# Computing 12 of 16 gate tiles inside two attention stages instead of in the matmul chains behind them

## What is computed

```python
# first block
proj = h @ w_in[layer]
p_rwkv, p_diff, p_gate = jnp.split(proj, [RWKV_COLS, RWKV_COLS + DIFF_COLS], axis=-1)
o_rwkv = rwkv7_mix(p_rwkv, ...) @ rwkv_w_o[layer]
o_diff = diff_attention(p_diff, ...) @ diff_w_o[layer]
gates = jax.nn.sigmoid(p_gate).reshape(bsz, seqlen, N_BRANCH, D_MODEL)
merged = gates[:, :, 0] * o_rwkv + gates[:, :, 1] * o_diff
h_res = h_res + merged @ w_out[layer]
# second block
o = nsa_attention(q, k_cmp, v_cmp, k_s, v_s, k_w, v_w, nsa_gates, rel_bias)
y = jax.nn.sigmoid(mg[..., :d]) * y_conv + jax.nn.sigmoid(mg[..., d:]) * y_attn
x = x + y @ w_out[i]
```

## Time and profile before

| | us |
|---|---|
| median of 3 runs | 3678.36 |
| lowest, highest | 3672.93, 3681.27 |
| profiled execution, its span | 3676.3 |

### The profile page before, as it was taken

The page is one execution under the profiler, slowest core; times in us unless marked ns, Lnnn a source line. Parts: engine busy times, 40 slices in busy tenths (PEclk is TensorE's granted clock), DMA queues, the critical chain, the costliest instruction groups (busy, mean ns, idle before and its releaser), DMA issues. The chain is left out here.

```text
span 3676.3 us, 57266 instructions
## 1 busy us (share of the span) xinstructions
PE 3363.3 (91%) x24193; PEld 2748.5 (75%) x24193; DVE 2025.1 (55%) x3289; ACT 1230.3 (33%) x2142; POOL 203.8 (6%) x171
## 2 busy tenths in 40 slices
PE   7978999988999999888999998978699889999998
PEld 6868888956888888656677776866578587878886
DVE  4875654565355344577546776356736545464342
ACT  4542332254334233214433222234412234233231
POOL 2213220010000000000000000000100020000000
PEclk9989998988999999989999999989799889999999
DMA  4431103201322222520122222312022003233231
GB/s 147 156 124 48 48 19 116 69 1 52 97 93 92 98 92 80 145 72 13 47 75 92 86 86 93 99 59 93 13 92 95 1 2 109 78 106 98 93 97 58
DMA packets 99462, 287.84 MB, mean 78 GB/s; under 512 B 19738, under 2 KB 23962, under 8 KB 97160
## 3 DMA queue, kind: packets, MB, share of 16 engines
q1 hardware_dynamic: 93104, 269.43, 22.6%
q10 hardware_dynamic: 6104, 14.75, 1.6%
HBM read 264.22 MB, written 19.89 MB: 77 GB/s over the span
## 5 line engine op out<-in xcount | busy, mean ns | idle before, releaser
L240 PE MATMUL acc<-h_hi,whi 128*128 128x512 f32 x1992 | 800.5, 402 | 65.4 <-DVE wlo L432 43.0
L240 PE MATMUL acc<-h_hi,wlo 128*128 128x512 f32 x1992 | 791.1, 397 | 0.0
L240 PE MATMUL acc<-h_lo,whi 128*128 128x512 f32 x1928 | 770.0, 399 | 0.0
L240 PEld LDWEIGHTS acc<-h_hi,whi 128*128 128x128 f32 x1992 | 379.1, 190 | 176.0 <-DVE wlo L432 45.3
L338 DVE TENSOR_TENSOR wlo<-wbuf,whi 128x1024 fp32r<-128x1024 f32 (+3 forms) x277 | 318.6, 1150 | 272.9 <-ACT whi L256 270.5
L240 PEld LDWEIGHTS acc<-h_hi,wlo 128*128 128x128 f32 x1992 | 379.3, 190 | 87.8
L240 PEld LDWEIGHTS acc<-h_lo,whi 128*128 128x128 f32 x1928 | 366.8, 190 | 86.2 <-issue 2.9
L256 ACT ACTIVATE whi<-wbuf 128x1024 fp32r<-128x1024 f32 (+3 forms) x277 | 274.5, 991 | 347.4 <-PE acc L240 318.3
L240 PE MATMUL acc<-arena_round,whi 128*128 128x512 f32 x736 | 236.6, 392 | 4.8 <-DVE arena_round L398 4.8
L338 DVE TENSOR_TENSOR wlo<-ahead,whi 128x1024 fp32r<-128x1024 f32 (+3 forms) x132 | 152.3, 1154 | 140.9 <-ACT whi L256 140.2
L256 ACT ACTIVATE whi<-ahead 128x1024 fp32r<-128x1024 f32 (+3 forms) x132 | 131.4, 995 | 174.7 <-PE acc L240 168.3
(11 more groups left out here) (748 smaller groups left out, 6265.7 us busy)
## 6 DMA issues: line engine op xcount, KB each, us to landing
wbuf<-in_mlp_out SPq DMA_DIRECT2D x46, 512.0 KB, 3.3
wbuf<-in_mlp_in SPq DMA_DIRECT2D x45, 512.0 KB, 3.3
wbuf<-in_w_gates SPq DMA_DIRECT2D x38, 512.0 KB, 3.4
wbuf<-in_ffn_up SPq DMA_DIRECT2D x29, 512.0 KB, 3.3
wbuf<-in_w_qkv SPq DMA_DIRECT2D x23, 512.0 KB, 3.4
rwkv_factors<-factors SPq DMA_DIRECT2D x8, 1320.0 KB, 4.6
ahead<-in_mlp_in SPq DMA_DIRECT2D x19, 512.0 KB, 3.4
wbuf<-in_w_rwkv SPq DMA_DIRECT2D x18, 512.0 KB, 5.7
```

The source lines that it names most:

```text
L240: mm = nc.tensor.matmul(acc[t % NB][:, 0:T], wt[s % ring][:, k - a, :], xt, start=(kx == 0 and q == 0), stop=(kx == job.K - 1 and q == 2))
```

## The change

A new class `Beside` computes the first 12 gate tiles of a block step by step inside the attention that comes before the chain. Its function `made(step)` says how many of the 12 x 24 matmuls are done by the end of a step: in `diff_attention` 12 in each swap step and 6 in each score step, in `nsa_attention` 6 in each step. Weight tiles are split in halves of 4 squares: high part by ACT, two or three steps ahead (`high`), low part by POOL (`low`). PE does its share (`pe`) right after the step's scores or swaps and before `turn` and `weigh`. Sums are in a single bank `acc`; the eviction, by ACT in block one and by DVE with the scale in block two, writes the gate without its sigmoid. SP loads through two places (`sp_first`, `sp`, `sp_last`), the last load being the first tile of the following chain. The chains keep four gate tiles each, and a side object `LateSigmoid` takes the 12 sigmoids, three in each of the first four slabs; DVE waits for all of them at slab 3. All `warm` calls of both attentions go. To make room for the bank, `diff_attention` gives up `ps_v` (values go through `ps_t`, with two more waits) and `nsa_attention` has three banks of scores instead of four. In SBUF, the gates lie over tiles of `p` and `z` that are no longer needed, `unscaled` lies in `o`, and five constants of the rwkv stage are freed earlier.

```diff
@@ -99,6 +99,106 @@
 def tile_list(ap):
...
+class Beside:
+    def __init__(self, nc, w, x, out, ahead, following, made, ring, scale=None):
+        self.nc, self.w, self.x, self.out, self.following, self.scale = nc, w, x, out, following, scale
+        self.place, self.first_loaded, self.times = ahead
+        self.made, self.N, self.R = made, len(out), ring
+        self.issued = self.split = self.lowered = self.kept = 0
+    def prepare(self, s):
+        self.wbuf = [self.place, s.sb("wbuf", [P, 8, P])]
+        self.whi, self.wlo = ([s.sb(n, [P, 4, P], F32R) for _ in range(self.R)] for n in ("whi", "wlo"))
+        self.acc = s.ps("acc", [P, BANK])
+        self.w_loaded = [s.sem("w_loaded") for _ in range(2)]
+        self.hi_ready, self.lo_ready, self.w_used, self.evicted = (s.sem(n) for n in ("hi_ready", "lo_ready", "w_used", "evicted"))
+    def sp_first(self, sp):
+        if self.times == 1:
+            sp.dma_start(self.wbuf[0][:], self.w[0, 0]).then_inc(self.first_loaded, 16)
+        sp.dma_start(self.wbuf[1][:], self.w[1, 0]).then_inc(self.w_loaded[1], 16)
+    def sp(self, sp, start, stop):
+        for n in range(start, stop):
+            sp.wait_ge(self.lo_ready, 2 * n - 2)
+            sp.dma_start(self.wbuf[n % 2][:], self.w[n, 0]).then_inc(self.w_loaded[n % 2], 16)
+    def sp_last(self, sp):
+        n = self.following.shape[3]
+        sp.wait_ge(self.lo_ready, 2 * self.N)
+        sp.dma_start(self.place[:, 0:n, :], self.following[0, 0]).then_inc(self.first_loaded, 16)
+    def pe(self, pe, step):
+        while self.issued < self.made(step):
+            n, k, q = self.issued // 24, self.issued % 24 // 3, self.issued % 3
+            h = 2 * n + k // 4
+            if n > 0 and k == 0 and q == 0:
+                pe.wait_ge(self.evicted, n)
+            if k % 4 == 0 and q == 0:
+                pe.wait_ge(self.lo_ready, h + 1)
+            wt = (self.whi, self.whi, self.wlo)[q][h % self.R]
+            mm = self.nc.tensor.matmul(self.acc[:], wt[:, k % 4, :], self.x[1 if q == 1 else 0][k], start=(k == 0 and q == 0), stop=(k == 7 and q == 2))
+            if k % 4 == 3 and q == 2:
+                mm.then_inc(self.w_used, 1)
+            self.issued += 1
+    def high(self, act, step):
+        while self.split < 2 * self.N and 12 * self.split < self.made(step):
+            h, n = self.split, self.split // 2
+            if h % 2 == 0:
+                act.wait_ge(*((self.first_loaded, 16 * self.times) if n == 0 else (self.w_loaded[n % 2], 16 * ((n + 1) // 2))))
+            if h >= self.R:
+                act.wait_ge(self.w_used, h - self.R + 1)
+            self.nc.scalar.activation(self.whi[h % self.R][:], self.wbuf[n % 2][:, 4 * (h % 2):4 * (h % 2) + 4, :], ACT.Copy).then_inc(self.hi_ready, 1)
+            self.split += 1
+    def low(self, pool, step):
+        while self.lowered < 2 * self.N and 12 * self.lowered < self.made(step):
+            h = self.lowered
+            pool.wait_ge(self.hi_ready, h + 1)
+            self.nc.gpsimd.tensor_tensor(self.wlo[h % self.R][:], self.wbuf[h // 2 % 2][:, 4 * (h % 2):4 * (h % 2) + 4, :],
+                                         self.whi[h % self.R][:].bitcast(F32), ALU.subtract).then_inc(self.lo_ready, 1)
+            self.lowered += 1
+    def complete(self, step):
+        while self.kept < self.N and 24 * (self.kept + 1) <= self.made(step):
+            self.kept += 1
+            yield self.kept - 1
+    def evict_scaled(self, dve, n):
+        dve.wait_ge(self.w_used, 2 * n + 2)
+        self.nc.vector.tensor_tensor(self.out[n], self.acc[:], self.scale[:], ALU.mult).then_inc(self.evicted, 1)
+    def evict(self, act, n):
+        act.wait_ge(self.w_used, 2 * n + 2)
+        self.nc.scalar.activation(self.out[n], self.acc[:], ACT.Copy).then_inc(self.evicted, 1)
+class LateSigmoid:
+    def __init__(self, nc, x, slabs):
+        self.nc, self.x, self.slabs = nc, x, slabs
+    def prepare(self, s_, evicted_d):
+        self.done = s_.sem("sigmoid_done")
+    def pe(self, pe, s, stat):
+        pass
+    def act(self, act, s):
+        if s < self.slabs:
+            N = len(self.x)
+            for t in self.x[N * s // self.slabs:N * (s + 1) // self.slabs]:
+                self.nc.scalar.activation(t, t, ACT.Sigmoid).then_inc(self.done, 1)
+    def dve(self, dve, s):
+        if s == self.slabs - 1:
+            dve.wait_ge(self.done, len(self.x))
@@ -1527,7 +1627,7 @@
-def diff_attention(nc, c, p, o, subln, busy):
+def diff_attention(nc, c, p, o, subln, beside):
@@ -1550,10 +1650,11 @@
-        unscaled, junk = s.sb("unscaled", [P, NA, P]), s.sb("junk", [P, P])
+        unscaled, junk = o.rearrange("p i (j d) -> p (i j) d", d=P), s.sb("junk", [P, P])
...
-        ps_t, ps_m, ps_o, ps_v = (s.ps(n, [P, BANK]) for n in ("ps_t", "ps_m", "ps_o", "ps_v"))
+        ps_t, ps_m, ps_o = (s.ps(n, [P, BANK]) for n in ("ps_t", "ps_m", "ps_o"))
+        beside.prepare(s)
@@ -1588,10 +1689,12 @@
             def _(sp):
...
+                beside.sp_first(sp)
+                beside.sp(sp, 2, beside.N)
+                beside.sp_last(sp)
...
             def _(pe):
-                warm(nc, ps_m, busy, 10)
@@ -1604,9 +1707,10 @@
                 def values(i):
...
+                        pe.wait_ge(wt_copied, NJ * i - 2)
...
                     for j in range(NJ):
-                        mm = nc.tensor.transpose(ps_v[:, j * P:(j + 1) * P], p[:, i + 16, M + j * P:M + (j + 1) * P], c["ident"][:])
+                        mm = nc.tensor.transpose(ps_t[:, j * P:(j + 1) * P], p[:, i + 16, M + j * P:M + (j + 1) * P], c["ident"][:])
@@ -1630,6 +1734,7 @@
+                    pe.wait_ge(vt_copied, min((a + 2) // NJ, 7) + 1)
@@ -1649,7 +1754,7 @@
                 def scaled(a):
...
-                    bank = (ps_t, ps_v)[i % 2]
+                    bank = (ps_t, ps_m)[i % 2]
@@ -1659,12 +1764,13 @@
-                for i, a, _, a2, a3 in lagging():
+                for u, (i, a, _, a2, a3) in enumerate(lagging()):
...
+                    beside.pe(pe, u)
@@ -1679,7 +1785,7 @@
-                    nc.scalar.activation(vt[b][:].rearrange("p j d -> p (j d)"), ps_v[:], ACT.Copy)
+                    nc.scalar.activation(vt[b][:].rearrange("p j d -> p (j d)"), ps_t[:], ACT.Copy)
@@ -1704,7 +1810,8 @@
-                for i, a, _, a2, a3 in lagging():
+                for u, (i, a, _, a2, a3) in enumerate(lagging()):
+                    beside.high(act, u + 2)
@@ -1713,22 +1820,28 @@
+                    for n in beside.complete(u):
+                        act.wait_ge(swap_ready, 2 * (n // 2) + 2)
+                        act.wait_ge(cos_done, 2 * (n // 2) + 2)
+                        beside.evict(act, n)
...
                 for i in range(8):
...
-                    nc.scalar.activation(o[:, i, :], (ps_t, ps_v)[i % 2][:], ACT.Copy, scale=weight[:, i:i + 1]).then_inc(written, 1)
+                    nc.scalar.activation(o[:, i, :], (ps_t, ps_m)[i % 2][:], ACT.Copy, scale=weight[:, i:i + 1]).then_inc(written, 1)
...
             def _(pool):
                 for i in range(8):
...
+                    beside.low(pool, 5 * i - 3)
...
+                beside.low(pool, 5 * 8)
@@ -2105,8 +2218,9 @@
-        ps_s = [[s.ps("ps_s", [P, BANK]) for _ in range(2)] for _ in range(2)]
+        ps_s = [s.ps("ps_s", [P, BANK]) for _ in range(3)]
...
+        beside.prepare(s)
@@ -2126,8 +2240,10 @@
             def _(sp):
+                beside.sp_first(sp)
                 for i in range(4):
...
+                        beside.sp(sp, 3 * i - 4, 3 * i - 1)
@@ -2136,6 +2252,8 @@
                         for b in range(8):
...
+                beside.sp(sp, 8, beside.N)
+                beside.sp_last(sp)
@@ -2144,13 +2262,13 @@
-                    for e in range(2):
-                        if p > 1:
-                            pe.wait_ge(top_ready[e], p - 1)
-                    warm(nc, ps_s[0][p % 2], busy, 14 if p == 0 else 4 if br == 2 else 1)
+                    if p > 1:
+                        pe.wait_ge(top_ready[1], p - 1)
+                    if p > 0:
+                        pe.wait_ge(top_ready[0], p)
                     for e in range(2):
...
-                        nc.tensor.matmul(ps_s[e][p % 2][:, 0:n], qs[rows(e), i, qi * P:(qi + 1) * P], k, start=True, stop=True).then_inc(sc_ready[e], 1)
+                        nc.tensor.matmul(ps_s[(2 * p + e) % 3][:, 0:n], qs[rows(e), i, qi * P:(qi + 1) * P], k, start=True, stop=True).then_inc(sc_ready[e], 1)
@@ -2197,6 +2315,7 @@
                 for p in range(NP + 6):
...
+                        beside.pe(pe, p)
@@ -2210,6 +2329,7 @@
             def _(act):
...
+                beside.high(act, 1)
@@ -2242,11 +2362,16 @@
                 for p in range(NP + 7):
...
+                        beside.high(act, p + 3)
...
+            @block.gpsimd
+            def _(pool):
+                beside.low(pool, NP)
@@ -2267,7 +2392,7 @@
```

(46 more changed lines are left out.)

4 lines of the change are left out of this document (2 added, 2 removed).

## The result

| | before | after |
|---|---|---|
| median of 4 runs (range) | 3677.7 us (3672.9 to 3681.3) | 3618.4 us (3615.7 to 3621.7) |
| ratio (95% interval) | | 0.984 (0.9826 to 0.9854) |
| span of the profiled execution | 3676.3 us | 3613.9 us |

The change makes the kernel 59 us faster. The forecast was 3624, its range 3600 to 3657.

What follows compares the result with a forecast made beforehand. The prediction took TensorE (PE), 91% busy, to bound the kernel. Its terms, -133.4 + 49 - 4 + 28 + 6.3 = -54 us, gave 3624 us, with a range of 3600 to 3657.

Steps and rivals of the forecast that it cites:

- Part 1: The two chains: twelve of sixteen gate tiles leave each, 66.7 us a chain, -133.4 us for two blocks.
- Part 2: Differential attention: 288 gate matmuls come in and partly fill PE's holes; stage 176.7 against 127.7 us, +49 (38 to 64).
- insertions: Differential attention: 40 breaks of PE's run of plain float matmuls, 0.1 us each, 4 us (0 to 8).
- cold clock: Opening of each attention stage: PE starts at a low clock, 3 us each (1.5 to 7 and 0 to 6).
- own work: PE's time in a stage without waits, tails, dummy matmuls and lost clock: 96 us in differential, 102.0 in selected attention.
- Part 3: Start of chain 1: with the new early weight load PE idles less before its first gate matmul, -4 us (-4.3 to -3.5).
- Part 4: Selected attention: gate matmuls replace dummy ones and fill waits; stage 179.7 against 151.5 us, +28 (19 to 41).
- Part 5: Chain 2: ConvNorm blocks ACT in slab 3, so PE waits 7.9 us instead of 1.6 before slab 6, +6.3 (4 to 9.5).
- Steps are chains: Both attention stages: no wait shrinks, since gates before turn and weigh pass their full length on; 3661 us, chance 0.12.
- Slower by 0.4 an insertion: Both attention stages: each of 88 insertions costs 0.4 us, 35 in place of 4; 3692 us, chance 0.04.
- Clean filling: Both attention stages: insertions, evictions and POOL cost nothing; 3602 us, chance 0.17.
- POOL on the path: Selected attention: 24 low parts hold DVE up by 0.6 us each, +11 on the forecast; 3635 us, chance 0.10.

Runs made afterwards that it cites:

- e2: The kernel after, with 8 of 16 gate tiles inside the attention stages instead of 12: 3617.2 us.
- e3: The kernel after, with 14 of 16 gate tiles inside the attention stages and ConvNorm one slab earlier: 3610.8 us.
- e8: The kernel after, with each step's gate matmuls in two places, the last three behind the turning: 3615.3 us.
- e5: The kernel after, with the accumulator's eviction ahead of the copy of turned weights in each step instead of behind it: 3618.5 us.
- e4: The kernel after, with ConvNorm's block in chain 2 taken apart: root in slab 3, reciprocal in 4, products and SiLUs in 4, 6, 8, 10: 3612.8 us.
- e7: The kernel after, with each of POOL's 48 low parts computed three times in a row: 3644.6 us.
- e9: The kernel after, with each step's gate matmuls behind turning and weighing instead of between scores and turning: 3629.6 us.
- e1: The kernel before, with the matmuls that only keep TensorE busy taken out of both attention stages: 3702.3 us.

## Why the prediction was right, point by point

- **PE is the bound, and its holes can be filled.** Right. e2 and e3 show where it ends: with 8 tiles the first stage is full (146.3 of 147.9 us busy), with 12 both nearly.
- **Part 1, -133.4.** The way from chain 1 to the selected attention lost 72.5: 66.7, the 5.1 of the fourteen `warm`, and 0.7. The way to the first GELU lost 59.6, which is 66.7 less the new stall of chain 2 (6.2) and 0.9.
- **Part 2, +49.** It was +44.7. To the point at which the forecast ended the stage, 1.1 later than my mark, it is 172.4 instead of 176.7. The terms behind PE's own work were mis-sized: insertions 4, measured 0 (e8); evictions 5, measured 1.9 in rows and 3.5 by e5; cold clock 3, measured 2 (4 us at 0.50); POOL 2, of which no wait over 0.4 is to be seen. These are some 8 too much. On the other side, "own work" of 96 was some 4 too small; where these lie is open. (Its two estimates, 97.4 and 94.4, should by their own terms read 97.8 and 94.6, which explains little of it.)
- **Part 3, -4.** PE's idle time before chain 1 fell by 3.8. The stretch as a whole lost 5.9. The rest is in the thin steps: 24.4 us with 18.5 busy at a clock of 0.72 before (861.6 to 886), 22.3 with 17.2 busy at 0.85 after (903.7 to 926.0). That clock differs from trace to trace, so this part is luck.
- **Part 4, +28.** It was +27.3 from the end of the opening matmuls (146.8 and 5.1 before, 179.2 after). Evictions 5, measured 4.4; cold clock 3, measured 1.6 (4 us at 0.60). Own work and POOL, 102.0 and 3 in the sum, measure 106.5 together and are not separated. DVE was to come to 116 us of busy time and came to 125: the 9 us of POOL's hold that the sum left out of DVE. The sum was right because errors of both signs met.
- **Part 5, +6.3.** The wait is 7.8, forecast 7.9; against 1.6 before that is +6.2, forecast +6.3. The three sigmoids ahead of the root take 1.66, and the rows are those that the prediction named. e4 shows what stands in ACT's block of 8.9 us: 3.35 of it is DVE's reciprocal, and taking the rest apart leaves a wait of 3.8.
- **What hides the moved work.** Halves split ahead: no wait for POOL's low parts in the kernel after; e7 shows that the lead is used up when they take three times as long. The shared `ps_t`: hidden, and e9 shows the price without the gate matmuls ahead.
- **The rivals.** *Steps are chains*: no; the waits of the two stages went from 33.5 to 7.7 us. *Slower by 0.4 an insertion*: no, by e8. *Clean filling*, 3602: the insertions are indeed free, but evictions aren't. Its three terms at nothing give 3605, not 3602, which is the case of all low ends. *POOL on the path*: the mechanism is real, and e7 turns it on (+22 us in the second stage); that its +11 did not come with each low part made once is shown by the stage's length, 179.2 against the 191 that it needs. My argument against it, "DVE has 60 us of air", was wrong as an argument: in e7 DVE has as much air, and PE waits.

The sum was -54, the touched stretches measured -61 (44.7 - 5.9 - 72.5 + 32.4 - 59.6 = -60.9), and the medians differ by 59.2. The forecast's error is nearly all in parts 2 and 3, +38.8 together instead of +45.

What I had not seen at all is the second half of why the change pays. I took `warm` in the selected attention for a cost with no use, 27 us to be subtracted. e1 says that without some filling the stage would be at 170. The gate matmuls are worth their time twice: as work, and as what holds the clock.

## What to carry to other kernels

Matmuls made only to keep TensorE busy mark a place where real, independent work can go; put it in small portions between scores and turning, where it covers the longest waits, and stop when PE's waits in the stage are gone, since the next tile then only changes place. Before calling a filling useless, take it out and look at the granted clock. Room on an engine is no proof that delays on it are free: ask what stands behind the delayed instruction in its fixed order.

## What the hardware showed beyond what I had expected

- PE busy for 18.9 of 20 us by its records, with short matmuls, was granted half clock (e1). The whole stage was at 0.64 with no filling, at 0.98 with the one or four 512-column `warm` matmuls a step, at 0.97 with four gate matmuls a step (e2) and at 0.99 with six.
- Going from plain float to rounded matmuls and back costs nothing measurable, 75 times more often (e8: -0.2 and -2.4 us in the stages), although the first rounded matmul of an insertion has its successor 0.34 us later and the others 0.23.
- POOL's hold on DVE's two-tile operations went with its load (some 9 us of DVE's busy time with 24 low parts, 26 with 72), but its price didn't: the stage of 179.2 us grew by 22.0, 10.2 of it waits and 11.9 busy time at a lower clock.
- A table load of ACT took 1.28 us, and the next function followed at once (1837.96 and 1839.25).
